# Latent attention of one core: value products of the last head pair cut from 512 to 128 query columns, and the last modulation product placed behind the last transposes

## What is computed

```python
s = jnp.einsum('bqhgd,bkhd->bhgqk', qblk, k).astype(jnp.float32) * scale
p = jax.nn.softmax(s, axis=-1).astype(v.dtype)
return jnp.einsum('bhgqk,bkhe->bqhge', p, v)
...
return o @ w_o
mod_s = jax.nn.silu(c) @ ada_w[l] + ada_b[l]
```

## Time and profile before

| | us |
|---|---|
| median of 3 runs | 1295.94 (1294.5 to 1296.41) |
| the profiled execution, its own time | 1293.82 |
| its span in the trace | 1292.0 |
| TensorE busy | 1225.8 (95%) |
| VectorE / ScalarE busy | 589.7 / 410.3 |
| mean granted TensorE clock | 0.989 |

### The profile page before, as it was taken

How to read it: one execution, slowest core, us unless ns; L and a number is a source line. 1 busy time by engine, 2 the same in 40 slices (tenths; PEclk the granted TensorE clock), 3 DMA queues, 4 the chain that set the end, 5 groups by cost and what they waited for, 6 DMA issues and landing times.

```text
span 1292.0 us, 16286 instructions
## 1 busy us (share of the span) xinstructions
PE 1225.8 (95%) x5081; PEld 660.6 (51%) x5082; DVE 589.7 (46%) x1338; ACT 410.3 (32%) x855; POOL 58.3 (5%) x63
## 2 busy tenths in 40 slices
PE   7999999999989999998968998899999999999996
PEld 4554555556644475443324444566654574444442
DVE  1322555555542574222318545887835662222216
ACT  2332444444441120111112326677722211111122
POOL 0103000000000020000011000000000110000002
PEclk9999999999999999999999999899999999999999
DMA  9979999522264067999976001500020369989946
GB/s 373 414 315 386 397 413 413 223 99 99 100 249 166 33 233 244 354 356 358 373 294 242 9 1 43 222 2 1 1 98 6 121 257 337 353 279 354 358 168 240
DMA packets 88353, 290.12 MB, mean 225 GB/s; under 512 B 9209, under 2 KB 27580, under 8 KB 86876
## 3 DMA queue, kind: packets, MB, share of 16 engines
q1 hardware_dynamic: 46032, 185.68, 39.2%
q0 software_dynamic: 16640, 64.59, 12.9%
q10 hardware_dynamic: 25612, 38.96, 8.9%
HBM read 214.48 MB, written 74.73 MB: 224 GB/s over the span
## 4 chain that ended last, share of the span: by engine, by line
PE 78%; DMA 7%; DVE 4%; ACT 4%; SPq 3%; issue 2%; ACTq 1%; DVEq 1%; POOLq 0%
PE ps L2135 15%; PE ps L1734 11%; PE ps L1751 11%; PE ps L1676 7%; PE ps L2164 6%; PE ps L2015 6%; PE ps L1978 4%; DMA arena<-in_moe_gu 4%; PE ps L1839 3%; PE ps L1785 3%; PE ps L2214 3%; PE ps L2077 2%; PE ps L1696 2%; PE ps L1988 2%; PE ps L1971 1%
## 5 line engine op out<-in xcount | busy, mean ns | idle before, releaser
L2135 PE MATMUL ps<-arena 128*128 (+1 forms) x560 | 246.3, 592 | 0.0
L1676 PE MATMUL ps<-const,arena 128*128 128x128 f32 (+2 forms) x1000 | 145.2, 278 | 23.6 <-DMA const<-in_const 8.0
L2135 PEld LDWEIGHTS ps<-arena 128*128 128x128 f32 x560 | 103.8, 190 | 117.3 <-issue 117.2
L1676 PEld LDWEIGHTS ps<-const,arena 128*128 128x128 f32 (+2 forms) x1000 | 115.2, 142 | 83.7 <-issue 46.2
L1734 PE MATMUL ps<-arena 128*128 128x512 f32 (+2 forms) x400 | 152.1, 535 | 4.6 <-DVE arena L1256 1.2
L1149 DVE TENSOR_REDUCE hst<-ps 128x1 f32<-128x640 f32 (+1 forms) x160 | 110.9, 714 | 85.8 <-PE ps L2015 71.7
L1751 PE MATMUL ps<-arena 128*128 128x512 f32 x320 | 142.0, 596 | 1.4 <-issue 1.4
L2164 PE MATMUL ps<-arena 128*128 (+1 forms) x280 | 126.1, 593 | 2.2 <-ACT arena L854 2.2
L730 ACT ACTIVATE arena<-ps,hst 128x640 f32<-128x640 f32 (+1 forms) x160 | 112.5, 707 | 42.3 <-DVE hst L1149 42.3
L1734 PEld LDWEIGHTS ps<-arena 128*128 128x128 f32 x400 | 74.4, 190 | 74.1 <-issue 57.9
L1751 PEld LDWEIGHTS ps<-arena 128*128 128x128 f32 x320 | 59.1, 190 | 70.4 <-issue 70.4
(11 more groups left out here) (220 smaller groups left out, 1147.2 us busy)
## 6 DMA issues: line engine op xcount, KB each, us to landing
arena<-in_moe_gu SPq DMA_DIRECT2D x128, 512.0 KB, 12.8
arena<-in_ada_w SPq DMA_DIRECT2D x62, 768.0 KB, 11.8
slot_rows<-arena POOLq DMA_DIRECT2D x10, 4096.0 KB, 67.0
arena<-in_moe_w_down SPq DMA_DIRECT2D x64, 512.0 KB, 16.4
slot_rows<-arena ACTq DMA_DIRECT2D x33, 512.0 KB, 8.9
arena<-slot_rows ACTq DMA_DIRECT2D x124, 128.0 KB, 13.4
arena<-mod_rows SPq DMA_DIRECT2D x12, 512.0 KB, 13.3
arena<-in_gqa_w_qkv SPq DMA_DIRECT2D x12, 512.0 KB, 13.8
```

Source lines behind the costliest of these rows:

```text
L1676: return nc.tensor.transpose(out, in_, ident[0:rows, 0:rows])
L2135: last = mm(bank(gu_bank(u)), e_xsT[:, nth(u, D)][:, k * P:(k + 1) * P], w(k * BANK, BANK), start=k == 0, stop=k == KD - 1)
```

## The change

It touches the programs of TensorE and ScalarE only. Pairs 0 to 6 keep their ten products of 512 columns. For pair 7 the ten products are issued once for each latent tile with 128 moving columns: `last_latents(1)` at loop index 76, `(2)` at 78, `(3)` at 80 and `(4)` at 82, each in its quarter of bank 6; only the last raises `pv_done`. The last modulation item goes from loop index 79 to 81, behind the transposes of step 79, on TensorE and on ScalarE. The third part of `mix` for tile 0, the first that writes bank 7, now waits until ScalarE has copied that item out.

```diff
-LATENTS_AT = ((2, 0, NB),)
+LATENTS_AT = 2
+LAST_ADA = STEPS + 1
...
                 if s < STEPS:
                     exp(0, s)
                     hook(0, *divmod(s, PER_PAIR))
+                if s == LAST_ADA:
+                    mod_out(ADA_ALL - 1)
...
             for j, at in zip(ada_in(l, m), ADA_AT):
-                if r == at:
+                if r == at and j < ADA_ALL - 1:
                     mod_out(j)
...
+            if l == 0 and it == 0 and part == 2:
+                pe.wait_ge(S("ada_out"), ADA_ALL)
...
+            def last_latents(it):
+
+                m = PAIR - 1
+                pe.wait_ge(S("pt_ready"), m * PER_PAIR + 2 * it + 2)
+                if it == 1:
+                    pe.wait_ge(S("oT_latent"), m)
+                for j in range(NB):
+                    for odd in range(2):
+                        at = j * BANK + (it - 1) * P
+                        last = mm(bank(6, P, (it - 1) * P)[VD * odd:VD * (odd + 1)], v_of(2 * m + odd, j), M_PT[odd][:, at:at + P],
+                                  start=j == 0, stop=j == NB - 1)
+                if it == LAT:
                     last.then_inc(S("pv_done"), 1)
...
-                for at, first, end in LATENTS_AT:
-                    if m and r == at:
-                        latents(m - 1, first, end)
+                if 0 < m < PAIR and r == LATENTS_AT:
+                    latents(m - 1)
+                if s % 2 == 0 and s >= (PAIR - 1) * PER_PAIR + 6:
+                    last_latents((s - 4 - (PAIR - 1) * PER_PAIR) // 2)
+                if s == LAST_ADA:
+                    spare_free(PAIR - 1, ADA_AT[1])
+                    ada(ADA_ALL - 1)
...
             for j, at in zip(ada_in(0, m), ADA_AT):
-                if r == at:
+                if r == at and j < ADA_ALL - 1:
                     spare_free(m, r)
                     ada(j)
```

More of the change, by code:

```diff
@@ L1775, in prompt, with latents @@
                 last.then_inc(S("pv_done"), 1)
[L1777 to L1783, removed]
+            def latents(m):
+                pe.wait_ge(S("pt_ready"), (m + 1) * PER_PAIR)
+                if m:
+                    pe.wait_ge(S("oT_latent"), m)
+                for j in range(NB):
                     for odd in range(2):
@@ L1786, in latents @@
                                   start=j == 0, stop=j == NB - 1)
-                if end == NB:
+                last.then_inc(S("pv_done"), 1)
+            def last_latents(it):
+                m = PAIR - 1
+                pe.wait_ge(S("pt_ready"), m * PER_PAIR + 2 * it + 2)
+                if it == 1:
+                    pe.wait_ge(S("oT_latent"), m)
+                for j in range(NB):
+                    for odd in range(2):
[3 more added lines that the diff above has]
+                if it == LAT:
                     last.then_inc(S("pv_done"), 1)
```

## The result

| | before | changed |
|---|---|---|
| median of 4 runs, us | 1295.75 (1294.5 to 1296.41) | 1288.45 (1288.28 to 1288.62) |
| profiled execution, its own time | 1293.82 | 1288.28 |
| span | 1292.0 | 1286.4 |
| mean granted clock | 0.989 | 0.994 |

The changed kernel takes 0.9945 of the time before, interval 0.9928 to 0.9962.

The account below looks back on a forecast made before the run. TensorE, busy 95% of the span, was taken as the bound. Without a clock fall, -1.2 us at the attention's end plus a 0.1 stall gave 1295.94 - 1.1 = 1294.8 us; 8-in-10 range 1292.6 to 1296.7.

Parts of the forecast that it names:

- the price of a block: Ten 128-column products take 1.1 us; with entering and leaving, about 1.4 us between full-width work.
- steps 1 to 5: End of attention 0, from the added blocks to `mix`: `mix` at 387.15 instead of 390.06, -2.9 us in the profiled execution.
- the clock's fall in before: TensorE's last value products of attention 0 ran at clock 0.51, costing 1.68 us; without this fall 1.2 us of gain remain.
- The rival of the weight loads: Narrow blocks: 64-column weight loads do not hide; +4.2 us with half hidden, at most about +9.6; chance 0.09.
- The stall of the modulation behind the attention: Layer 1's modulation fetches start 0.4 us later relative to `mix`; stall booked at 0.1 us, bounds 0 and 1.
- step 6: Behind the attention everything moves along with the same events, except later modulation fetches, booked as a 0.1 us stall.
- I take it in 4 of 10 executions: Share of executions of the kernel before in which the clock falls at the end of attention 0; median without it likelier.
- The first rival: End of attention 0: the clock's fall was in the compared runs and goes; -2.8 us, 1293.1; chance 0.25.
- the border of 1.95 and 2.57 us: TensorE pauses elsewhere: one of 1.95 us left the clock at 1.00, one of 2.57 brought it to 0.50.

Follow-up runs that it names:

- again: Kernel before and changed kernel each rerun with one number written another way, every instruction as it was: 1.0003 and 0.9940 of the kernel before.
- item alone: Kernel before with only the last modulation item moved, last pair's value products still 512 wide: 1294.35 us, 0.9989 of before.
- changed with 34 products: Changed kernel with 34 unused products (136 instructions) added in TensorE's pause at 669 us: 1292.42 us, 0.9973 of the kernel before.
- blocks alone: Changed kernel with the last modulation item back at its old place, only the split into 128-column blocks kept: 1289.19 us, 0.9951 of before.
- before with 120 and with 30: Kernel before with 120 empty instructions (1295.45 us, 1.0001) or 30 unused products (1292.72 us, 0.9976) added in TensorE's pause at 669 us.
- new order: Changed kernel with item at index 79 on TensorE, tile 1 at 80, tiles 2 and 3 together at 81, tile 4 at 82: 1286.80 us, 0.9932 of before.

## Why the prediction was wrong

**Right: the price of a block and the chain, steps 1 to 5.** Each event came within 0.3 us of its forecast:

| event | forecast | measured |
|---|---|---|
| scores of step 79 | 378.15 | 378.26 |
| transposes of step 78 | 381.0 | 381.23 |
| copy of step 78 | 381.8 | 382.03 |
| transposes of step 79 | 382.9 | 383.17 |
| the item | 383.6 | 383.86 |
| last block | 385.0 | 385.27 |
| `mix` | 387.15 | 387.42 |

Two blocks ahead of the scores cost 2.71 us together (booked 2.6): the scores of step 77 are 1.28 later, those of step 79 another 1.43. With the clock's fall in before, the piece is 2.6 us shorter (said 2.9), without it 17.58 - 16.69 = 0.9 (said 1.2). The rival of the weight loads fell: 20 loads and 20 products of alternating halves in 1.24 us leave no excess. By the Trainium skill, "TensorE: Matmul & The Clock Gate", Part 3, loads overlap only where the row group differs. The trace does not agree: all rows were used here, and the loads hid. In the loop a block cost 1.28 and 1.43 us, more than its 1.1 us of columns. That agrees with the Trainium skill, "TensorEngine Tiling (Array Packing)", Key Properties, by which a change of the tiling mode drains TensorE; no run takes the drain apart from other costs of a block. The stall of the modulation behind the attention was not there: VectorE ended it at 400.64, TensorE came to it at 401.32.

**Wrong, first: "Behind the attention all is tied to the same events and moves along" (step 6).** It held for what the change moves in time: the pieces up to the last sums differ by 0.2 us. It did not hold for where TensorE's loads of instructions fall. Every instruction that follows stood 120 places further in a code that arrives 256 at a time, and the load that had fallen into the last store came some 20 us earlier. The four runs with 120, 136 and again 120 and 136 added instructions switched the end between 34.2 to 34.5 and 37.4 to 39.7 us in both kernels. The mean of the end over all profiles with the norm row in its old place is 38.1 us with the load in the store (before, again, item alone, changed with 136 empty ones, changed with 34 products) and 34.4 without (changed, again, blocks alone, before with 120 and with 30, new order): **3.7 us that the sum had at nothing** (3.3 without the one of 39.67, where the clock was down longest; 3.1 between the two compared profiles). No rival covered it either, as all were at the place of the change. The prediction could have asked for it: the order shows 120 instructions more, and the view of DMAs of before has the load in the store.

**Wrong, second: "I take it in 4 of 10 executions".** The clock fell at the end of attention 0 in 5 of 6 profiles of kernels whose order there is that of before (all but the one with 120 empty instructions, which come later in the program), and in none of the four with the changed order (changed, again, with 136 empty ones, with 34 products). The first rival, with its 1.7 us, was the likelier case. The reason given for the small chance, the profiled time 2.1 below the median, was weak: executions differ elsewhere too. The pieces up to step 76 and from `mix` to `mix` vary by 2 us each between profiles, in both kernels (370.7 to 372.7; 560.9 to 563.0 where no empty instructions are in them). Four profiles of the fourteen, of before and of the changed kernel, had the clock down at 105 us. These four have the second product of step 76 at 372.5 to 372.7, the other ten at 370.7 to 371.0. Nor does the length of one pause decide, as the border of 1.95 and 2.57 us had it: behind the last gathers 2.75 and 2.82 us brought the clock down, 2.95 and 3.11 did not.

**The sum after the fact.** 2.6 at the changed place and 3.7 at the end are 6.3 us, against 7.3 (4 runs each) and 7.0 (13 and 4 runs) between the medians. In the two profiled executions, 2.6 + 3.1 - 0.1 = 5.6 is the whole difference of the spans. About 1 us of the medians stays open: runs of before spread by up to 6.7 us and those of the change by 3.8 at most. Falls of the clock at places that the change does not touch, as at 105 us, have a part in that, and two profiles of each kernel do not tell how often they come.

## What to carry to other kernels

The 120 instructions moved every later load of TensorE's code. Before giving a price to a change that adds or removes instructions, look in the view of DMAs for an instruction packet beside a transfer on which the end hangs, and test it by adding as many harmless instructions in a pause. Then a gain or a loss far from the edit can be told from the edit's own, and the more durable cure is to take away what makes the coincidence costly (here by fetching the norm row early), since the place of the load changes with the next edit. For added work of narrow blocks: put it behind the last item that feeds another engine, where the engine waits anyway.

## What was not expected of the hardware

- One instruction packet of 16 KB inside the landing of a 512 KB store went with 3.3 us instead of 2.6 for the store and 7.9 to 8.6 instead of 4.8 to 5.1 for the gather behind it. With the norm row out of the way it was 5.8 with the packet and 4.9 without.
- The clock's answer to the same pauses (1.84 and 0.79 us around a transpose of 0.75) was both 0.51 and 1.00, in executions with the same instructions up to that place; with 0.88 and 0.88 it fell already at 380. Single pauses of 2.95 and 3.11 us left it at 1.00, one of 2.75 brought it down.
- An empty instruction that raises a semaphore is not free on TensorE: 120 of them filled a pause of 15.25 us and 136 one of 17.53 us, 0.13 us each. The pauses ended with them, and not with the gather that had ended one of 10.9 us.
